# Shifted copies of a depthwise convolution through device memory: one store and four loads a tile for sixteen copies

## The reference

```
def depthwise_conv(u, w, b, pad):
    y = lax.conv_general_dilated(u, w[:, None, :], (1,), (pad,), ..., feature_group_count=u.shape[-1])
    return y + b

def conformer_conv(va, vg, p):
    u = va * jax.nn.sigmoid(vg)
    u = depthwise_conv(u, p["conv_w"], p["conv_b"], (15, 15))     # 31 taps, one filter for each channel
    return jax.nn.silu(layernorm(u, p["ln_g"], p["ln_b"]))
...
z = h @ p["w_in"];  va, vg, ga, xb, gb = split(z)
y_a = conformer_conv(va, vg, p) * silu(ga)
y_b = rglru_branch(xb, ...) * silu(gb)                            # gates, exponentials and a scan over time
```

## Time and profile before

| | |
|---|---|
| median of 3 runs | 1043.34 us (1043.27 to 1047.85) |
| the profiled execution | 1048.97 us |
| its span | 1047.2 us |
| TensorE busy | 934.9 us (89%) |
| VectorE busy | 709.7 us (68%) |
| ScalarE busy | 503.4 us (48%) |
| GpSimd busy | 105.8 us (10%) |
| q1, SyncE's DMAs: share of the sixteen engines | 44.1% |
| q0, GpSimd's DMAs: share of the sixteen engines | 13.1% |
| the 128 copies, GpSimd issuing them | 62.9 us, 499 ns each |

### The profile page before, as it was taken

How to read it: one execution, slowest core, us unless ns; L and a number is a source line. 1 busy time by engine, 2 the same in 40 slices (tenths; PEclk the granted TensorE clock), 3 DMA queues, 4 the chain that set the end, 5 groups by cost and what they waited for, 6 DMA issues and landing times.

```text
span 1047.2 us, 17178 instructions
## 1 busy us (share of the span) xinstructions
PE 934.9 (89%) x7056; PEld 867.5 (83%) x7056; DVE 709.7 (68%) x1057; ACT 503.4 (48%) x725; POOL 105.8 (10%) x212
## 2 busy tenths in 40 slices
PE   5699997877998998988987889968979989999996
PEld 3488765767998998878977889968869889999996
DVE  3985779738665899958567885465378596656453
ACT  3625889495555553143443265355142444444441
POOL 0005856300000001101002200000000000000000
PEclk9799999889998999999999899988889989999999
DMA  9736988643363778838609834333235556665661
GB/s 376 283 117 183 326 256 283 237 121 101 112 230 103 224 230 307 308 101 302 193 1 361 302 101 121 107 115 85 77 101 161 161 188 187 185 183 184 187 205 53
DMA packets 55872, 195.27 MB, mean 186 GB/s; under 512 B 7921, under 2 KB 9073, under 8 KB 54386
## 3 DMA queue, kind: packets, MB, share of 16 engines
q1 hardware_dynamic: 40178, 147.57, 44.1%
q0 software_dynamic: 15616, 46.61, 13.1%
HBM read 188.44 MB, written 1.05 MB: 181 GB/s over the span
## 4 chain that ended last, share of the span: by engine, by line
PE 57%; DVE 19%; DMA 10%; ACT 6%; issue 4%; POOL 2%; SPq 1%; DVEq 0%; ACTq 0%; POOLq 0%
PE ps L510 17%; PE ps L511 16%; PE ps L512 16%; DMA modw<-in_mod_w 6%; DVE w_lo L1235 4%; DVE modw L1269 2%; DMA m<-in_mod_w 2%; ACT w_hi L871 2%; PE px L474 2%; POOL shifts L443 2%; DMA raw<-in_stream 2%; DVE dump L1590 1%; DVE t L1255 1%; PE ps L578 1%; PE px L567 1%
## 5 line engine op out<-in xcount | busy, mean ns | idle before, releaser
L1235 DVE TENSOR_TENSOR w_lo<-raw,w_hi 128x1024 fp32r<-128x1024 f32 x232 | 280.2, 1222 | 177.4 <-ACT w_hi L871 176.6
L510 PE MATMUL ps<-h_hi,w_hi 128*128 128x256 f32 (+1 forms) x928 | 280.6, 302 | 43.4 <-DVE w_lo L1235 27.8
L871 ACT ACTIVATE w_hi<-raw 128x1024 fp32r<-128x1024 f32 x232 | 243.4, 1055 | 146.6 <-DMA raw<-in_stream 146.6
L511 PE MATMUL ps<-h_lo,w_hi 128*128 128x256 f32 (+1 forms) x928 | 275.9, 297 | 0.0
L512 PE MATMUL ps<-h_hi,w_lo 128*128 128x256 f32 (+1 forms) x928 | 275.3, 297 | 0.0
L510 PEld LDWEIGHTS ps<-h_hi,w_hi 128*128 128x128 f32 x928 | 184.2, 199 | 54.6 <-DVE w_lo L1235 36.0
L511 PEld LDWEIGHTS ps<-h_lo,w_hi 128*128 128x128 f32 x928 | 184.7, 199 | 3.4 <-issue 0.7
L512 PEld LDWEIGHTS ps<-h_hi,w_lo 128*128 128x128 f32 x928 | 184.1, 198 | 2.7
L510 PE MATMUL ps<-h2o_hi,w_hi 128*128 128x256 f32 x352 | 108.4, 308 | 30.5 <-DVE w_lo L1235 14.0
L434 POOL DMA_DIRECT2D modw<-in_mod_w x80 | 42.8, 536 | 671.6 <-DVE modw L1269 402.4
L511 PE MATMUL ps<-h2o_lo,w_hi 128*128 128x256 f32 x352 | 105.3, 299 | 0.0
(11 more groups left out here) (302 smaller groups left out, 1729.6 us busy)
## 6 DMA issues: line engine op xcount, KB each, us to landing
raw<-in_stream SPq DMA_DIRECT2D x252, 512.0 KB, 3.7
modw<-in_mod_w POOLq DMA_DIRECT2D x80, 512.0 KB, 6.3
m<-in_mod_w SPq DMA_DIRECT2D x8, 1024.0 KB, 16.2
shifts<-upad POOLq DMA_DIRECT2D x128, 35.5 KB, 5.3
c_row<-in_c_rows SPq DMA_DIRECT2D x3, 512.0 KB, 6.2
ctxT<-in_ctxT SPq DMA_DIRECT2D x1, 1024.0 KB, 5.1
x<-in_xT SPq DMA_DIRECT2D x1, 1024.0 KB, 7.1
ctx2T<-in_ctx2T SPq DMA_DIRECT2D x1, 1024.0 KB, 6.9
```

Source lines behind the costliest of these rows:

```text
L510: pe.matmul(o, wh, hi, start=start, stop=False)
L511: pe.matmul(o, wh, lo, start=False, stop=False)
L871: act.activation(w_hi[split[0] % HI_RING][:], raw[n % RING][:], ACT.Copy).then_inc(w_hi_ready, 1)
L1235: v.tensor_tensor(w_lo[n % RING][:], raw[n % RING][:], w_hi[split[0] % HI_RING][:].bitcast(F32), ALU.subtract).then_inc(w_lo_ready, 1)
```

## The change

A tensor in device memory, `u_rows`, takes the gated tile with its padding, 128 rows of 288 numbers (144 KB). GpSimd stores it with one DMA (a semaphore of its own for each tile, `u_stored`), waits until it has landed, and loads each channel group with one DMA over all 128 partitions whose source overlaps: 4 shifts, 32 rows, 284 numbers, a step of one number between shifts. The wait for the convolution of tile t - 2 now stands behind the store. TensorE's wait counts four loads in place of sixteen copies. ScalarE's wait for `upad` of tile t - 3 is now for its store.

```
+        u_stored = [sem(f"u_stored{t}") for t in range(KT)]
...
+        u_rows = nc.dram_tensor("u_rows", (KT, P, UW), F32, kind="Internal")
...
                 pool.wait_ge(u_gated, t + 1)
+                pool.dma_start(u_rows.ap()[t], upad[:, t % 3, :]).then_inc(u_stored[t], 16)
                 if t >= 2:
                     pool.wait_ge(tile_done, TILE[("cv", t - 2)] + 1)
+                pool.wait_ge(u_stored[t], 16)
                 for g in range(4):
-                    for d in range(4):
-                        pool.dma_start(shifts[t % 2][32 * d:32 * d + 32, g, :],
-                                       upad[32 * g:32 * g + 32, t % 3, d:d + RW]).then_inc(shifts_in[t % 2], 16)
+                    pool.dma_start(shifts[t % 2][:, g, :],
+                                   bass.AP(u_rows, (t * P + 32 * g) * UW, [[1, 4], [UW, 32], [1, RW]])) \
+                        .then_inc(shifts_in[t % 2], 16)
...
-                pe.wait_ge(shifts_in[t % 2], 256 * (t // 2 + 1))
+                pe.wait_ge(shifts_in[t % 2], 64 * (t // 2 + 1))
...
-                    act.wait_ge(shifts_in[(t - 3) % 2], 256 * ((t - 3) // 2 + 1))
+                    act.wait_ge(u_stored[t - 3], 16)
```

## The result

| | before | after |
|---|---|---|
| median of the runs made together | 1044.21 us (1039.06 to 1050.79, 6) | 1056.99 us (1052.4 to 1058.7, 6) |
| ratio to before | 1 | 1.0107, interval 1.0066 to 1.0149 |
| profiled execution | 1048.97 us | 1057.81 us |
| its span | 1047.2 us | 1056.0 us |
| first gate product (L572, before L567) to the end of the last convolution | 126.7 us | 132.1 us |

The kernel became 1.07% slower (1.22% by the two medians); I had said no difference, 1043.6 us, and 1047.3 at most. Of the 8.8 us between the two profiled executions 5.4 lie in the stretch that the copies touch, 0.7 before it and 2.7 behind it. Of these 2.7 the granted clock accounts for 2.0: behind the stretch it cost 46.5 us before and 48.5 after. The loads stand at L447, and all lines behind them are numbered five higher than before.

What follows compares the result with a forecast made beforehand. TensorE, busy 89% of the span, was taken as the bound, with five waits (11.0 us) for VectorE's weight splits. The terms -1.39 + 1.39 + 0.3 made +0.3 us, 1043.34 to 1043.6 us, range 1039.7 to 1047.3.

Steps and rivals of the forecast that it cites:

- rival D: Loads confined to few DMA engines, the same four each time, delay weight tiles and modulation loads: 1073 us; chance 0.08.
- the rest, costed at nothing: Tiles 1 to 5 and 7, later modulation groups, ScalarE's buffer wait and DMA engine load: no cost to TensorE.
- Step 1: Tile 0, group 1: GpSimd free 3.6 us sooner, so TensorE's 1.39 us wait at 113 us vanishes.
- Step 2: Tile 6, group 5: the store's wait drains the queue, giving back 1.39 us and making TensorE 0.3 us later.
- the rule of the queue in the prediction: GpSimd's queue: a store behind modulation loads can't land before them; tile 6's was to land at 174.0 to 176.1 us.
- B: Group 1's landing is bound by DMA crowding, not its issue, so the 1.39 us gain is missing: 1045.0 us; chance 0.10.
- C: Tile 6's store takes 10.8 us in crowded engines, so group 5 lands up to 4.9 us late: 1048.2 us; chance 0.14.
- E: Shorter TensorE waits let three slow blocks run at full clock, 4.9 us on top of 1.39: 1037.0 us; chance 0.06.

Runs made afterwards that it cites:

- direct_4: Kernel before with four copies a tile straight from SBUF, channel first over sixteen engines, no store or wait: 0.9951 of before, 1039.89 us.
- loads_16_alone: loads_alone with the source walked channel first, so its loads go over sixteen engines; convolution values not the reference's: 0.9942 of before, 1041.45 us.
- direct_4_wait: direct_4 with the store and GpSimd's wait for it put back before its four copies, which still read SBUF: 1.0013 of before.
- loads_16_engines: Changed kernel with each load's source walked channel first, over sixteen engines, shifted buffer and weights numbered to match: 0.9992 of before, 1044.97 us.
- loads_alone: Changed kernel without store and wait; its four-engine loads read other data from device memory, convolution values not the reference's: 1.0032 of before.
- store_no_wait: loads_alone with the store issued too, GpSimd not waiting for it; convolution values not the reference's: 1.0044 of before.
- group_ahead_16: Changed kernel with sixteen-engine loads and, at tiles 0 and 6, the modulation group issued before GpSimd's wait: 0.9955 of before, 1039.33 us.
- group_ahead: Changed kernel, four-engine loads kept, with the modulation group issued before GpSimd's wait at tiles 0 and 6: 1.0081 of before, 1053.66 us.

## Why the prediction was wrong, point by point

**The parts as measured**, each by its own pair of kernels:

| part | pair | time | stretch |
|---|---|---|---|
| four transfers for sixteen | before to direct_4; before to loads_16_alone | -0.5%; -0.6% | -7.1 us; -7.2 us |
| store and wait, sixteen engines | direct_4 to direct_4_wait; loads_16_alone to loads_16_engines | +0.6%; +0.5% | +7.2 us; +3.5 us |
| store and wait, four engines | loads_alone to after | +0.75% | +7.4 us |
| four engines, with the wait | loads_16_engines to after | +1.15% | +9.1 us |
| four engines, without it | loads_16_alone to loads_alone | +0.9% | +5.2 us |

The way from before over loads_16_alone and loads_16_engines to after has the steps -0.58, +0.50 and +1.15%, which are the +1.07%. Of the two causes neither makes the loss by itself once the issues are saved: with the wait alone the kernel stands at 0.9992 and 1.0013, with the four engines alone at 1.0032.

In every kernel the stretch is made of two things, TensorE's waits of over 0.3 us and its busy time. The matmuls are the same, so the busy time differs with the granted clock, which in these traces is either at the full or at half of it:

| kernel | waits, us | busy, us | mean granted clock |
|---|---|---|---|
| before | 11.0 | 115.7 | 0.95 |
| after | 17.5 | 114.7 | 0.94 |
| loads_alone | 10.1 | 114.6 | 0.96 |
| store_no_wait | 12.3 | 113.2 | 0.96 |
| direct_4 | 7.3 | 112.3 | 0.97 |
| direct_4_wait | 11.1 | 115.7 | 0.95 |
| loads_16_engines | 8.3 | 114.7 | 0.96 |
| loads_16_alone | 7.1 | 112.4 | 0.97 |
| group_ahead_16 | 7.2 | 112.5 | 0.97 |

The two steps that end in the changed kernel, 9.1 and 7.4 us, are all waits. In the other pairs two fifths to two thirds are the clock, and a difference of 2 or 3 us between two stretches may be one slow block more or less.

**The step that failed** is the one behind rival D: "on four different sets of four each engine has the same share as now, and only a load's own way is longer", with its companion in "the rest, costed at nothing", that the DMA engines' load "stays nearly the same". The Trainium skill (DMA: Bandwidth & Descriptors, Why a DMA increments its semaphore by 16 and not by 1) has four engines and a cursor that goes round, and the trace agrees as far as it can, since it names no engine: the first load of tile 0 starts with four packets at once at 96.9 us, four more join them at 97.6 while they are under way, and around 172 us up to twenty are in flight. So the sets rotated, as forecast. What I drew from it was wrong. A packet of a load, 4544 bytes, is under way for 336 ns on average with four engines and for 220 ns with sixteen in the same kernel, so the 1024 of them take 344 us of packet time in place of 226 (the old copies, 2048 of 123 ns: 252), and the share of the engines' time that GpSimd's queue takes from 84 to 225 us is 44.7% in place of 36.5. The fastest packets take 173 ns in both kernels: it isn't that a packet costs more on four engines, but that two thirds of them are held up (fewer than a third with sixteen). And what lies behind the loads lands later: the median landing of `raw` was 5.8 us against 4.6, of `modw` 9.5 against 8.2. That such a tile needs all sixteen engines and so waits for the slowest is my reading of it, not shown. I had priced the load's own way and not that of the transfers that share its engines. D was right that the confined loads delay the rest and wrong about the condition: it doesn't need the four sets to coincide. The price of that is 1.15% with the wait and 0.9% without it.

What these pairs don't separate: exchanging the two dimensions also changes the order in which the rows are read, which of them share a packet, the 16-byte packets and the length of the issue (0.5 us a tile). No run has sixteen engines with the old order or four with the new.

**Step 1** (gain of 1.39 us) came out as a loss of 4.02 at that wait. Issue and wait of the store took 3.4 us instead of 2.1, the four loads 2.75 instead of 2.1, and the start was 0.8 us later, so GpSimd was free at 98.2 instead of 95.5; then the landing took 15.30 us instead of 9.64. The first part is two terms mis-sized by 1.9 us together, and the start; the second is the failed step above: over sixteen engines the same landing took 10.9 us. There GpSimd was free 5.1 us after the store's issue began (in the change 6.1, forecast 4.2), and the wait at 113 was gone: step 1 held in its result. In direct_4_wait, where group 1 landed at 110.2, it did not. The forecast was also short on the other side: it let the saved issues give 1.39 us, and four transfers for sixteen gave 5 to 6.

**Step 2** (tile 6 gives the gain back) held for GpSimd and not for TensorE. GpSimd sat 10.60 us between store and loads where I had said 7 and more, and the store landed 0.4 us behind group 4, as the rule of the queue in the prediction has it. Group 5 went out from 188.8, far from the 176 to 178 that I had named, because all before it was late. TensorE's wait behind group 5 didn't grow, it shrank from 3.23 to 1.37 us. The large wait came one place earlier, behind group 4.

**The rest, costed at nothing** was the second mis-sized term. I had looked at each tile's convolution, which starts long after its copies, and found slack there; and TensorE never waits for the loads in the changed kernel, which is right. Two things were missing. One is the way of group 4 through the crowded engines, 2.6 us longer, behind which stands the wait of 7.57 us. The other is GpSimd's own slack: I had written that at all other places "GpSimd itself waits for VectorE or TensorE" and taken it for a sign that nothing there could be late. The store waits of tiles 1 to 5, 47.1 us by the rows above, used it up. In the changed kernel that cost nothing yet, because VectorE was late by as much; in group_ahead, where VectorE was not, it took away what the better order had won.

**The rivals.** B (crowding sets group 1's landing) and C (the wait costs more) were both partly true, and at 1048.2 C was still too cheap: it counted one tile. E, the clock, came to little in the change: the blocks behind 117.92 and 192.54 ran at granted clocks of 0.71 and 0.69, between the two levels of 1.2 and 2.4 GHz, those behind 175.37 and 209.44 at 1.00, so two slow blocks, 2.1 and 2.3 us over their 6.1, stand where three had cost 4.9 us. In the faster kernels it did come: 3.4 of the 7.1 us of direct_4 are E's.

```profile
117.90:126.10 8.20, 8.18 (x52) 8.05 (x56) 5.79 (x7) 5.30 (x8) 3.83 (x7) 0.71 0.86 255
...
175.30:181.50 6.20, 6.13 (x52) 5.97 (x56) 2.55 (x5) 6.17 (x10) 0.14 (x1) 1.00 1.03 408
192.50:200.90 8.40, 8.36 (x52) 8.23 (x56) 6.60 (x10) 3.55 (x6) 0.76 (x2) 0.69 0.94 321
```

## What to carry to other kernels

When a queue issues work and waits for a landing, cost the wait at every place where it stands, with landing times from the busy stretch and behind what is ahead in the same queue, and set the sum against the queue's own idle time; a consumer that starts late doesn't show that slack. Then look who waits for what goes out late: here groups 2 and 3 went out 8 to 10 us late and nobody was waiting. Put what others need soon ahead of the wait, not behind it. And read the slowest dimension of each new access pattern: if it is small, price the transfer by the engines that it holds back for everybody else, or exchange two dimensions, which here was worth 1.15% for one line and a permuted weight. And split a gain in TensorE's time into waits and busy time before explaining it: half of some of these was the granted clock.

## What the runs showed of the hardware that I had not expected

- The loads with 4 as their slowest dimension have 3072 packets of 16 bytes in the changed kernel, 96 for each of 32 loads, which the kernels with 32 don't have. That would be eight for each of the twelve engines left out; the trace doesn't name them. GpSimd takes 691 ns on average to issue such a load and 566 ns for one over sixteen.
- The same 4544 bytes took 318 to 371 ns on average as a packet on four engines (371 where the loads ran without the store) and 203 to 265 ns on sixteen, and 173 ns at best on either. What holds the packets up isn't settled. The store is excluded by loads_alone; the crowding of four engines, the small packets and the order of the rows can't be told apart by these runs.
- A store of 144 KB landed in 3.1 us in an empty queue and in up to 15 us behind a modulation group, in the changed kernel 0.4 to 0.8 us after the group's last load each time. On SyncE's queue six of eight took 5.9 to 9.3 us.
- A busy share of the DMA engines near 1.00 went with 368 GB/s before and 191 GB/s after, in the same three microseconds: the share doesn't tell how much is moved.
